# Query latents and attention's output gates with both input parts as one moving operand, and a convolution gate and its values in one weight group

## The chip, the cores and the metric

The kernel runs on one core of one Trainium2 chip. Its time is the device time of one execution in microseconds (us); several executions are run and their median is given. Five engines with queues of their own work side by side: TensorE (PE in the rows; PEld is its weight loads), VectorE (DVE), ScalarE (ACT), GpSimd (POOL, unused here) and SyncE (SP), which only issues DMAs.

## What is computed

Two blocks on 256 tokens of 2048 channels, all in float32. The first (attention with a recurrence, then an MLP) is not touched. The second has two layers, and each does this:

```python
z = h @ w_in[l]
q_lat, kv_lat, k_rope, mla_gate, conv_in, conv_gate = jnp.split(z, splits, axis=-1)
q = (rms_norm(q_lat, q_lat_g[l]) @ w_q_up[l]).reshape(b, s, N_HEADS, QK_DIM)
kv = (rms_norm(kv_lat, kv_lat_g[l]) @ w_kv_up[l]).reshape(b, s, N_HEADS, NOPE_DIM + V_DIM)
...
attn = causal_block_attention(q, k, v).reshape(b, s, D_MLA)
mla_out = attn * jax.nn.silu(mla_gate)
u_val, u_gate = jnp.split(conv_in + glu_b[l], 2, axis=-1)
u = u_val * jax.nn.sigmoid(u_gate)
u = causal_depthwise_conv(u, dw_w[l], dw_b[l])
u = jax.nn.silu(layer_norm(u, conv_ln_g[l], conv_ln_b[l]))
u = u @ w_pw[l] + b_pw[l]
conv_out = u * jax.nn.silu(conv_gate)
y = jnp.concatenate([mla_out, conv_out], axis=-1) @ w_out[l]
x = x + gate * y
```

q_lat has 512 channels (4 tiles of 128), mla_gate 1024 (8 tiles), u_gate and u_val 1024 each, conv_gate 1024; the convolution has 31 taps.

## The kernel before

Every float32 product is made of three: a number is split into a high part that TensorE takes exactly and the rest, and `high*high + high*low + low*high` is summed in PSUM. The input's parts are `HT[:, kt, 0]` and `HT[:, kt, 1]` (`HTh`, `HTl`); a weight's parts are `WH` and `WL`.

**Halves.** Weights arrive in chunks of up to 1 MB. Each chunk is worked on in halves of up to 128x1024 numbers, and the half is the unit of the whole kernel. ScalarE makes `WH` (line 1922), VectorE makes `WL = RAW - WH` (line 1084, called the split of that half here), TensorE multiplies. There are four buffers for each part, so the high part of half n+4 can begin when TensorE has finished half n. There are 636 halves in all and 130 in each layer of the second block; halves are numbered 0 to 129 within a layer here, also for the changed kernel.

**Two ways of multiplying.** `products` with `cols=4` (lines 578 to 580) has a half of 2 input tiles x 4 output tiles and issues three matmuls of 256 columns for each of these 8 pairs. `joint_products` (lines 630, 632) has 4 input tiles x 2 output tiles, and issues one matmul of 512 columns (both input parts against `WH`) and one of 256 (`HTh` against `WL`) for each pair. The two input parts then lie in two stretches of a bank, and have to be added: ScalarE copies one to SBUF (`second_part`, line 2570), and VectorE adds the other (`summed`, line 1080), 2 operations of 256 columns for each group of 2 tiles.

**The order of a layer** (`weight_course`): group of convolution gates 0 to 3 (halves 0 to 7), values 0 to 3 joint (8 to 15), key and value latents (16 to 23), query latents (24 to 31), `w_kv_up` (32 to 35), convolution gates 4 to 7 (36 to 43), their values (44 to 51), `w_q_up` (52 to 57, three groups of two halves), attention's output gates (58 to 73), the convolution's output gates joint (74 to 89), half of `w_out2` (90 to 97), `w_pw`, the rest of `w_out2`. Groups take two pairs of PSUM banks in turn, so a group's first matmul waits for whoever reads the group two before it.

**Side work** is cut into steps, the strands. `Course.beat` runs one step of every strand behind each half, on each engine by the same count: TensorE's step stands behind its half n, while VectorE's and ScalarE's step n stands ahead of their work for half n+4. So VectorE does step n between its splits of halves n+3 and n+4. The strands: `convolution` (VectorE's taps, line 1443, 3 or 4 to a step by `tap_steps`, and one start per tile by ScalarE, line 2142), `key_latents`, `query_latents`, `heads` (norms and rotation of keys and queries), `attend` (26 steps) and `channel_norm` (15 steps, starts when both convolution strands have ended). TensorE's small products of the strands take four further banks in turn (`small_bank`), and each waits until the reader of the bank's last content is done.

`glued` (line 1820) is VectorE's gated values: it reads a group of values in PSUM, adds the bias and multiplies by the gate. It releases the banks (`taken`).

## Time and profile before

| | |
|---|---|
| median of 3 executions | 1962.79 us (1962.68 to 1963.76) |
| the profiled execution | 1963.59 us, its span 1961.8 us |
| TensorE busy | 1939.5 us, 99% of the span |
| VectorE busy | 1525.5 us, 78% |
| ScalarE busy | 1069.1 us, 54% |
| granted TensorE clock | 1.0 throughout (2.4 GHz) |
| chain that ended last | 96% TensorE |

The profiler's span leaves out 1.8 us around the work. Shares are means over stages that differ: a layer of the second block takes about 409 us, the first from 1139 us and the second from 1548 us, and in some of its stretches VectorE is as busy as TensorE. The start of a ScalarE row on line 1922 that ended a wait for PE tells when TensorE finished the half four before it.

### The profile page before, as it was taken

To read this page: it belongs to the slowest core of one execution; us is meant where nothing else is said; L and a number is where in the kernel's file an instruction comes from. 1 tells how busy PE (TensorE), PEld (TensorE's weight loads), DVE (VectorE), ACT (ScalarE), POOL (GpSimd) and SP (SyncE) were. 2 spreads that over 40 slices of the span, in tenths; PEclk is the share of its full clock that TensorE was granted. 3 is DMA by queue.
4 is the path that set the end of the run, shared out by engine and by line. 5 is a ranking of instruction groups with operands and counts; after the bars stand their busy time and mean duration, and the time that the engine had idled before them with its cause. 6 is when DMAs were issued, how large, how long until landed. Compare 5 with 4: busy or idle time off the path is not lost.

```text
span 1961.8 us, 27925 instructions
## 1 busy us (share of the span) xinstructions
PE 1939.5 (99%) x11546; PEld 1683.0 (86%) x11546; DVE 1525.5 (78%) x2092; ACT 1069.1 (54%) x1545; POOL 0.2 (0%) x4
## 2 busy tenths in 40 slices
PE   7999999999999999999999999999999999999999
PEld 6888888888888888888888889999888899998887
DVE  6587776868887777888877567999966669999764
ACT  5474766465664433555543475554764566456742
POOL 0000000000000000000000000000000000000000
PEclk9999999999999999999999999999999999999999
DMA  7443445938889888989898734544455455454453
GB/s 283 153 164 124 139 151 200 358 134 296 332 337 335 331 332 331 340 321 338 330 334 331 254 125 165 187 168 139 163 188 181 147 193 173 151 172 135 172 194 123
DMA packets 63982, 442.59 MB, mean 226 GB/s; under 512 B 7248, under 2 KB 7536, under 8 KB 12400
## 3 DMA queue, kind: packets, MB, share of 16 engines
q1 hardware_dynamic: 61920, 434.30, 61.9%
q10 hardware_dynamic: 1936, 6.51, 1.0%
q8 instruction: 91, 1.49, 0.3%
q14 instruction: 35, 0.29, 0.0%
HBM read 438.67 MB, written 2.11 MB: 225 GB/s over the span
## 4 chain that ended last, share of the span: by engine, by line
PE 96%; DVE 2%; ACT 1%; DMA 0%; issue 0%; ACTq 0%; DVEq 0%
PE PS L630 22%; PE PS L632 11%; PE PS L509 11%; PE PS L511 11%; PE PS L510 11%; PE PS L578 7%; PE PS L579 7%; PE PS L580 7%; PE PS L501 6%; PE PS L657 1%; DMA X<-in_x 0%; DVE WL L1084 0%; DVE Y L1126 0%; ACT S L1985 0%; ACT WH L1922 0%
## 5 line engine op out<-in xcount | busy, mean ns | idle before, releaser
L1922 ACT ACTIVATE WH<-RAW 128x1024 fp32r<-128x1024 f32 (+1 forms) x636 | 663.6, 1049 | 752.3 <-PE PS L511 282.5
L1084 DVE TENSOR_TENSOR WL<-RAW,WH 128x1024 fp32r<-128x1024 f32 (+1 forms) x636 | 766.4, 1209 | 374.7 <-ACT WH L1922 373.4
L630 PE MATMUL PS<-HT,WH 128*128 128x512 f32 x1912 | 678.5, 398 | 0.0
L632 PE MATMUL PS<-HT,WL 128*128 128x256 f32 x1912 | 535.8, 280 | 0.0
L630 PEld LDWEIGHTS PS<-HT,WH 128*128 128x128 f32 x1912 | 358.6, 188 | 88.8 <-issue 7.2
L632 PEld LDWEIGHTS PS<-HT,WL 128*128 128x128 f32 x1912 | 361.3, 189 | 0.1
L578 PE MATMUL PS<-HT,WH 128*128 128x256 f32 x1008 | 291.2, 289 | 0.7 <-DVE HT L1135 0.4
L580 PE MATMUL PS<-HT,WL 128*128 128x256 f32 x1008 | 285.5, 283 | 0.0
L579 PE MATMUL PS<-HT,WH 128*128 128x256 f32 x1008 | 285.5, 283 | 0.0
L1093 DVE SCALAR_TENSOR_TENSOR RAW<-RAW,CB 128x2048 f32<-128x2048 f32 x96 | 219.3, 2284 | 0.0
L511 PE MATMUL PS<-WH,Ul 128*128 128x512 f32 x512 | 203.0, 396 | 0.0
L509 PE MATMUL PS<-WH,Uh 128*128 128x512 f32 x512 | 202.5, 396 | 0.0
L578 PEld LDWEIGHTS PS<-HT,WH 128*128 128x128 f32 x1008 | 193.4, 192 | 10.6 <-issue 7.8
L510 PE MATMUL PS<-WL,Uh 128*128 128x512 f32 x512 | 201.2, 393 | 0.0
L1443 DVE SCALAR_TENSOR_TENSOR UG<-UV,PK,UG 128x256 f32<-128x256 f32 x480 | 200.4, 478 | 0.2
L579 PEld LDWEIGHTS PS<-HT,WH 128*128 128x128 f32 x1008 | 193.6, 192 | 0.4
L580 PEld LDWEIGHTS PS<-HT,WL 128*128 128x128 f32 x1008 | 193.5, 192 | 0.0
L510 PEld LDWEIGHTS PS<-WL,Uh 128*128 128x128 f32 x512 | 96.1, 188 | 23.8
L511 PEld LDWEIGHTS PS<-WH,Ul 128*128 128x128 f32 x512 | 96.1, 188 | 23.7
L509 PEld LDWEIGHTS PS<-WH,Uh 128*128 128x128 f32 x512 | 96.1, 188 | 22.5
L509 PE MATMUL PS<-WH,HT 128*128 128x512 f32 x256 | 100.8, 394 | 0.0
L511 PE MATMUL PS<-WH,HT 128*128 128x512 f32 x256 | 99.8, 390 | 0.0
(317 smaller groups left out, 2026.7 us busy)
## 6 DMA issues: line engine op xcount, KB each, us to landing
RAW<-in_w_in SPq DMA_DIRECT2D x112, 1024.0 KB, 4.8
RAW<-in_ada_w SPq DMA_DIRECT2D x96, 1024.0 KB, 6.3
RAW<-in_w_up SPq DMA_DIRECT2D x64, 1024.0 KB, 5.8
RAW<-in_w_down SPq DMA_DIRECT2D x64, 1024.0 KB, 5.7
RAW<-in_w_out SPq DMA_DIRECT2D x48, 1024.0 KB, 4.8
RAW<-in_w_pw SPq DMA_DIRECT2D x8, 1024.0 KB, 4.8
RAW<-in_w_in SPq DMA_DIRECT2D x8, 768.0 KB, 4.2
RAW<-in_w_q_up SPq DMA_DIRECT2D x6, 1024.0 KB, 4.8
```

What stands on the lines that cost most here:

```text
L509: e.matmul(out, sh, mh, start=st, stop=False, skip_group_check=True)
L510: e.matmul(out, sh, ml, start=False, stop=False, skip_group_check=True)
L511: return e.matmul(out, sl, mh, start=False, stop=final, skip_group_check=True)
L578: e.matmul(out, sh, ah, start=first and i % 2 == 0, stop=False, skip_group_check=True)
L579: e.matmul(out, sh, al, start=False, stop=False, skip_group_check=True)
L580: op = e.matmul(out, sl, ah, start=False, stop=final, skip_group_check=True)
L630: e.matmul(bk[i][:, 0:512], wh[:, at], m["HT"][:, kt, :, :].rearrange("p a t -> p (a t)"), start=kt == 0, stop=False, skip_group_check=True)
L632: op = e.matmul(bk[i][:, 0:256], wl[:, at], HTh[:, kt, :], start=False, stop=kt == n.kts - 1, skip_group_check=True)
L1084: e.tensor_tensor(m[f"WL{j % NHL}"][:, 0:nk * w], m[f"RAW{i % NRAW}"][:, k0 * w:(k0 + nk) * w], m[f"WH{j % NHL}"][:, 0:nk * w].bitcast(F32 ...
L1093: e.scalar_tensor_tensor(raw[:, :], raw[:, :], 1.0, m["CB"][:, :], ALU.mult, ALU.mult, accum_out=mod[:, k:k + 1]).then_inc(signals["ada"], 1)
L1443: e.scalar_tensor_tensor(UG[:, c, :], UV[:, c, j:j + 256], dw[:, c, j:j + 1], UG[:, c, :], ALU.mult, ALU.add).then_inc(signals[name], 1)
L1922: e.activation(m[f"WH{j % NHL}"][:, 0:nk * w], m[f"RAW{i % NRAW}"][:, k0 * w:(k0 + nk) * w], ACT.Copy).then_inc(signals["high"], 1)
```

## The change

The input weights of a layer are grouped anew. A group of 512 columns now holds the gates of two channel tiles and the values of the same two (`GLU`, groups 0, 6 and 7); tiles 2 and 3 have two joint groups, gates and values (`GLU_JOINT`). The query latents are two joint groups in place of one plain group of four tiles, attention's output gates four joint groups in place of two plain ones. The number of halves stays, and so do their bytes. The parts of a joint group are added by `second_part` and `summed` as before. The convolution's first strand starts behind half 8 instead of behind half 16, with tiles 0 and 1, and takes up 2 and 3 from its turn 7; the second starts behind half 44 instead of 52, with tiles 4 and 5, and takes up 6 and 7 from its turn 10. The channel norm's step 10 waits until the last input product is through.

```diff
-GLU_VALUES, GLU_GATES, Q_LATENT, KV_LATENT, MLA_GATES, CONV_GATES = ((0, 1), 5), (2, 6), 3, 4, (7, 8), (9, 10, 11, 12)
-LAYER_JOINT = GLU_VALUES[0] + CONV_GATES
+GLU, GLU_JOINT, Q_LATENT, KV_LATENT, OUT_GATES = (0, 6, 7), (1, 2), (3, 4), 5, tuple(range(8, 16))
+LAYER_JOINT = GLU_JOINT + Q_LATENT + OUT_GATES
...
     def tap_steps(self, L, c0):
-        yield range(4)
-        n, turn = 4, 0
-        while n < 124:
-            k = min(3 if c0 == 0 and turn < SLOW_TURNS else 4, 124 - n)
-            yield range(n, n + k)
-            n, turn = n + k, turn + 1
+        later = 7 if c0 == 0 else 10
+        done = [0] * 4
+        for turn in range(99):
+            taps = []
+            if turn in (1, later):
+                taps = [(0, c0 + c) for c in ((0, 1) if turn == 1 else (2, 3))]
+            for _ in range(3 if c0 == 0 and later < turn <= later + SLOW_TURNS else 4):
+                c = min(range(4 if turn > later else 2), key=lambda c: done[c])
+                if turn > 1 and done[c] < 30:
+                    done[c] += 1
+                    taps.append((done[c], c0 + c))
+            yield taps
+            if sum(done) == 120:
+                return
...
@@ tensor_program
-        for g in GLU_VALUES[0]:
+        taps = [course.start(convolution(L, 0))]
+        for g in GLU_JOINT:
             joint_products(group[f"w_in2_{L}", g], h)
-        taps = [course.start(convolution(L, 0))]
         products(group[f"w_in2_{L}", KV_LATENT], *hidden, h, cols=3)
         side_k = course.start(key_latents(L))
-        products(group[f"w_in2_{L}", Q_LATENT], *hidden, h, cols=4)
+        for g in Q_LATENT:
+            joint_products(group[f"w_in2_{L}", g], h)
...
-        for g in (GLU_GATES[1], GLU_VALUES[1]):
-            products(group[f"w_in2_{L}", g], *hidden, h, cols=4)
+        products(group[f"w_in2_{L}", GLU[1]], *hidden, h, cols=4)
         taps.append(course.start(convolution(L, 4)))
+        products(group[f"w_in2_{L}", GLU[2]], *hidden, h, cols=4)
...
-        for g in MLA_GATES:
-            products(group[f"w_in2_{L}", g], *hidden, h, cols=4)
-        for g in CONV_GATES:
+        for g in OUT_GATES:
             joint_products(group[f"w_in2_{L}", g], h)
+        flags.add(("inputs", L))
...
@@ vector_program
+        def glued(g, c0, gates):
             n = group[f"w_in2_{L}", g]
+            dve.wait_ge("half_done", n.done)
+            dve.wait_ge("uz", L + 1)
+            dve.wait_ge("u_sig", 4 * L + gates)
+            for c in range(c0, c0 + 2):
+                op = e.scalar_tensor_tensor(UV[:, c, 30:286], bank[2 * n.pair + 1][:, 256 * (c - c0):256 * (c - c0) + 256],
+                                            pk(f"glu_b{L}")[:, c:c + 1], UG[:, c, :], ALU.add, ALU.mult)
+            op.then_inc(signals["taken"], 1)
...
+        n = group[f"w_in2_{L}", GLU[2]]
+        for j, _ in course.begin(n):
+            if j == n.first + 1:
+                glued(GLU[1], 4, 3)
         norm = course.start(channel_norm(L, taps))
         course.drain(side_q)
         for g in range(3):
-            course.group(group[f"w_q_up_{L}", g])
+            n = group[f"w_q_up_{L}", g]
+            for j, _ in course.begin(n):
+                if g == 0 and j == n.first + 1:
+                    glued(GLU[2], 6, 4)
...
@@ scalar_program
-        for k, g in enumerate(CONV_GATES):
+        for k, g in enumerate(OUT_GATES):
             n = group[f"w_in2_{L}", g]
             for j, _ in course.begin(n):
-                if k == 2 and j == n.first + 2:
-                    gates_done(0)
-            second_part(n, CG[:, 2 * k:2 * k + 2, :])
+                if k and k % 2 == 0 and j == n.first + 2:
+                    gates_done(k // 2 - 1)
+            second_part(n, (MG, CG)[k // 4][:, 2 * (k % 4):2 * (k % 4) + 2, :])
```

**First place: VectorE around the start of `w_q_up`.** `UV<-PS,PK,UG` is `glued`, `UG<-UV,PK,UG` the taps, `WL<-RAW,WH` the splits. Before, the first row is the split of half 54:

```order
L1084 TENSOR_TENSOR WL<-RAW,WH 128x1024 [waits high]
L1820 SCALAR_TENSOR_TENSOR UV<-PS,PK,UG 128x256 [waits stored,uz,half_done]
L1820 SCALAR_TENSOR_TENSOR UV<-PS,PK,UG 128x256 x3
L1443 SCALAR_TENSOR_TENSOR UG<-UV,PK,UG 128x256 [waits taps0] x4
L1084 TENSOR_TENSOR WL<-RAW,WH 128x1024 [waits high] x2
```

In the changed kernel, the second split here is that of half 56 and the last that of half 57:

```order
L1095 TENSOR_TENSOR WL<-RAW,WH 128x1024 [waits high]
L1460 SCALAR_TENSOR_TENSOR UG<-UV,PK,UG 128x256 [waits taps1] x4
L1095 TENSOR_TENSOR WL<-RAW,WH 128x1024 [waits high]
L1837 SCALAR_TENSOR_TENSOR UV<-PS,PK,UG 128x256 [waits u_sig,half_done]
L1837 SCALAR_TENSOR_TENSOR UV<-PS,PK,UG 128x256
L1460 SCALAR_TENSOR_TENSOR UG<-UV,PK,UG 128x256 [waits taps1] x4
L1095 TENSOR_TENSOR WL<-RAW,WH 128x1024 [waits high]
```

The gated values that free a pair of banks for the second group of `w_q_up` stood behind the split of half 54 and now stand behind that of half 56; on TensorE the group that waits for them begins with half 54 in both.

**Second place: VectorE where the queries' heads end and attention begins.** `QN<-QN,PK,PS` and `QP<-QP,PS` are the last two steps of `heads`, `S<-PS,CN` and `MX<-S` attention's scores. Before (the second split is that of half 71, the last that of 72):

```order
L1525 SCALAR_TENSOR_TENSOR QN<-QN,PK,PS 128x512 [waits h_wide]
L1528 TENSOR_TENSOR QP<-QP,PS 64x256 x2
L1443 SCALAR_TENSOR_TENSOR UG<-UV,PK,UG 128x256 [waits taps1] x4
L1084 TENSOR_TENSOR WL<-RAW,WH 128x1024 [waits high]
L1525 SCALAR_TENSOR_TENSOR QN<-QN,PK,PS 128x512 [waits h_wide]
L1528 TENSOR_TENSOR QP<-QP,PS 64x256 x2
L1548 SCALAR_TENSOR_TENSOR S<-PS,CN 128x384 [waits a_score] x2
L1554 TENSOR_REDUCE MX<-S 128x1 [waits a_in]
L1554 TENSOR_REDUCE MX<-S 128x1
L1443 SCALAR_TENSOR_TENSOR UG<-UV,PK,UG 128x256 [waits taps1] x4
L1084 TENSOR_TENSOR WL<-RAW,WH 128x1024 [waits high]
```

and in the changed kernel:

```order
L1091 TENSOR_TENSOR Y<-PS,Y 128x256 [waits joint_low] x2
L1542 SCALAR_TENSOR_TENSOR QN<-QN,PK,PS 128x512 [waits h_wide]
L1545 TENSOR_TENSOR QP<-QP,PS 64x256 x2
L1460 SCALAR_TENSOR_TENSOR UG<-UV,PK,UG 128x256 [waits taps1] x4
L1095 TENSOR_TENSOR WL<-RAW,WH 128x1024 [waits high]
L1542 SCALAR_TENSOR_TENSOR QN<-QN,PK,PS 128x512 [waits h_wide]
L1545 TENSOR_TENSOR QP<-QP,PS 64x256 x2
L1565 SCALAR_TENSOR_TENSOR S<-PS,CN 128x384 [waits a_score] x2
L1571 TENSOR_REDUCE MX<-S 128x1 [waits a_in]
L1571 TENSOR_REDUCE MX<-S 128x1
L1460 SCALAR_TENSOR_TENSOR UG<-UV,PK,UG 128x256 [waits taps1] x4
L1095 TENSOR_TENSOR WL<-RAW,WH 128x1024 [waits high]
```

Two sums of a joint group (`Y<-PS,Y`) stand there besides all that stood there before; the same pair comes in ahead of the splits of halves 67, 71, 75 and 79.

**Third place: TensorE where the channel norm begins.** `PS<-UG,CN` is its first sum, `PS<-CN,S` and `PS<-VT,V` are a step of attention. Before, behind half 83:

```order
L632 MATMUL PS<-HT,WL 128x256
L501 MATMUL PS<-UG,CN 32x256 [waits taps1,taps0]
L501 MATMUL PS<-UG,CN 32x256 x7
L630 MATMUL PS<-HT,WH 128x512 [waits split]
```

and in the changed kernel, behind half 76:

```order
L641 MATMUL PS<-HT,WL 128x256
L925 MATMUL PS<-CN,S 128x128 [waits a_probs,a_pt]
L925 MATMUL PS<-CN,S 128x128 x2
L510 MATMUL PS<-VT,V 128x256 [waits a_out]
L510 MATMUL PS<-VT,V 128x128
L510 MATMUL PS<-UG,CN 32x256 [waits taps1,taps0,a_in]
L510 MATMUL PS<-UG,CN 32x256 x7
L639 MATMUL PS<-HT,WH 128x512 [waits split]
```

The norm's sum moved ahead by seven halves, into the middle of attention's steps, and it now takes the bank of a pair of scores: it waits for `a_in`, VectorE's reading of the fifth head's scores (`S<-PS,CN`), which stands behind the split of half 79.

## Rows read from the trace of the kernel before

**Rows 1.** The page's first part: busy time, share of the span and instructions.

```profile
PE 1939.5 (99%) x11546; PEld 1683.0 (86%) x11546; DVE 1525.5 (78%) x2092; ACT 1069.1 (54%) x1545; POOL 0.2 (0%) x4
```

**Rows 2.** The page's fourth part: the chain that ended last, by engine.

```profile
PE 96%; DVE 2%; ACT 1%; DMA 0%; issue 0%; ACTq 0%; DVEq 0%
```

**Rows 3.** Windows of the first layer; PE, PEld, DVE, ACT, POOL busy, clock, DMA.

```profile
1229.00:1268.00 39.00, 39.00 (x293) 35.29 (x292) 35.84 (x63) 22.66 (x31) 0.00 (x0) 1.00 0.61 212
1268.00:1308.00 40.00, 40.00 (x330) 38.97 (x330) 39.69 (x74) 16.66 (x21) 0.00 (x0) 1.00 0.41 142
1309.00:1413.00 104.00, 104.00 (x762) 93.84 (x761) 103.72 (x207) 61.00 (x104) 0.00 (x0) 1.00 0.45 154
```

**Rows 4.** Timeline of PE, query latents as plain products: start, us, operation.

```profile
1223.70 0.28 PE L578 MATMUL PS<-HT,WH 128*128 128x256 f32 x1
1223.82 0.28 PE L579 MATMUL PS<-HT,WH 128*128 128x256 f32 x1
1223.94 0.28 PE L580 MATMUL PS<-HT,WL 128*128 128x256 f32 x1
1224.06 0.28 PE L578 MATMUL PS<-HT,WH 128*128 128x256 f32 x1
```

**Rows 5.** Timeline of PE in a joint group (values 2 and 3).

```profile
1189.55 0.39 PE L630 MATMUL PS<-HT,WH 128*128 128x512 f32 x1
1189.78 0.28 PE L632 MATMUL PS<-HT,WL 128*128 128x256 f32 x1
1189.90 0.39 PE L630 MATMUL PS<-HT,WH 128*128 128x512 f32 x1
```

**Rows 6.** Timeline of DVE behind half 15: two sums, and the split of 19.

```profile
1194.77 0.79 DVE L1080 TENSOR_TENSOR UV<-PS,UV 128x256 f32<-128x256 f32 x2 [1.39 <-ACT UV L2570]
...
1196.20 0.95 DVE L1084 TENSOR_TENSOR WL<-RAW,WH 128x768 fp32r<-128x768 f32 x1
```

**Rows 7.** Timeline of DVE ahead of half 41's split: split of 40, then keys' rotation.

```profile
1253.77 1.23 DVE L1084 TENSOR_TENSOR WL<-RAW,WH 128x1024 fp32r<-128x1024 f32 x1 [0.58 <-ACT WH L1922]
...
1257.63 0.34 DVE L1499 TENSOR_SCALAR KV<-KV,PK 128x256 f32<-128x256 f32 x1
```

**Rows 8.** Timeline of ACT there: TensorE has finished halves 38 and 39.

```profile
1258.37 1.06 ACT L1922 ACTIVATE WH<-RAW 128x1024 fp32r<-128x1024 f32 x1 [2.48 <-PE PS L580]
...
1262.36 1.06 ACT L1922 ACTIVATE WH<-RAW 128x1024 fp32r<-128x1024 f32 x1 [2.41 <-PE PS L580]
```

**Rows 9.** Timeline of DVE around `w_q_up`'s start: gated values, splits of 55, 56.

```profile
1302.80 1.22 DVE L1084 TENSOR_TENSOR WL<-RAW,WH 128x1024 fp32r<-128x1024 f32 x1
1304.05 1.66 DVE L1820 SCALAR_TENSOR_TENSOR UV<-PS,PK,UG 128x256 f32<-128x256 f32 x4
1305.62 1.67 DVE L1443 SCALAR_TENSOR_TENSOR UG<-UV,PK,UG 128x256 f32<-128x256 f32 x4
1307.20 1.22 DVE L1084 TENSOR_TENSOR WL<-RAW,WH 128x1024 fp32r<-128x1024 f32 x1
1308.81 1.23 DVE L1084 TENSOR_TENSOR WL<-RAW,WH 128x1024 fp32r<-128x1024 f32 x1 [0.38 <-ACT WH L1922]
```

**Rows 10.** Timeline of ACT there: TensorE has finished halves 51 and 55.

```profile
1300.89 1.06 ACT L1922 ACTIVATE WH<-RAW 128x1024 fp32r<-128x1024 f32 x1 [1.76 <-PE PS L580]
...
1312.41 1.06 ACT L1922 ACTIVATE WH<-RAW 128x1024 fp32r<-128x1024 f32 x1 [0.78 <-PE PS L580]
```

**Rows 11.** Timeline of DVE: split of half 72, split of 79 and the scores behind it.

```profile
1366.15 1.22 DVE L1084 TENSOR_TENSOR WL<-RAW,WH 128x1024 fp32r<-128x1024 f32 x1
...
1388.19 1.22 DVE L1084 TENSOR_TENSOR WL<-RAW,WH 128x1024 fp32r<-128x1024 f32 x1
1389.33 1.01 DVE L1548 SCALAR_TENSOR_TENSOR S<-PS,CN 128x384 f32<-128x384 f32 x2
```

**Rows 12.** Timeline of ACT: TensorE has finished halves 68, 76 and 78.

```profile
1360.02 1.06 ACT L1922 ACTIVATE WH<-RAW 128x1024 fp32r<-128x1024 f32 x1 [4.38 <-PE PS L580]
...
1388.93 1.06 ACT L1922 ACTIVATE WH<-RAW 128x1024 fp32r<-128x1024 f32 x1 [0.97 <-PE PS L632]
...
1395.46 1.06 ACT L1922 ACTIVATE WH<-RAW 128x1024 fp32r<-128x1024 f32 x1 [1.23 <-PE PS L632]
```

**Rows 13.** Timeline of PE: attention's step behind half 76, then half 77 begins.

```profile
1388.67 0.49 PE L916 MATMUL PS<-CN,S 128*128 128x128 f32 x3
1388.99 0.82 PE L501 MATMUL PS<-VT,V 128*128 128x256 f32 x4
1389.57 0.48 PE L630 MATMUL PS<-HT,WH 128*128 128x512 f32 x1
```

More of the change, by code:

```diff
@@ L933, in channel_norm @@
         for n in range(15):
+            while n == 10 and ("inputs", L) not in flags:
+                yield
             if n == 0:
                 b = small()
-                pe.wait_ge("taps0", 124 * L + 124)
-                pe.wait_ge("taps1", 124 * L + 124)
+                pe.wait_ge("taps0", 120 * L + 120)
+                pe.wait_ge("taps1", 120 * L + 120)
                 spread_sum(b, lambda i: UG[:, i, :]).then_inc(signals["n_sum"], 1)
@@ L1582, in channel_norm @@
         for n in range(15):
+            while n == 10 and ("inputs", L) not in flags:
+                yield
             if n in (0, 2, 6, 8):
@@ L1795, in vector_program @@
         UV, UG = m["UV"], m["UG"]
-        CG = Y[:, 1, :].rearrange("p (h t) -> p h t", h=8)
+        MG, CG = (Y[:, i, :].rearrange("p (h t) -> p h t", h=8) for i in range(2))
         def summed(g, part):
@@ L1826, in vector_program @@
         course.pace = 1
-        course.group(group[f"w_in2_{L}", GLU_GATES[0]])
+        course.group(group[f"w_in2_{L}", GLU[0]])
         course.pace = 99
-        a, b = GLU_VALUES[0]
+        taps = [course.start(convolution(L, 0))]
+        a, b = GLU_JOINT
+        n = group[f"w_in2_{L}", a]
+        for j, _ in course.begin(n):
+            if j == n.first + 1:
+                glued(GLU[0], 0, 1)
+        n = group[f"w_in2_{L}", b]
+        for j, _ in course.begin(n):
+            if j == n.first + 1:
+                summed(a, UG[:, 2:4, :])
+            if j == n.done - 1:
+                summed(b, UV[:, 2:4, 30:286])
+                gated()
@@ L1830, in vector_program @@
+        course.group(group[f"w_in2_{L}", KV_LATENT])
+        side_k = course.start(key_latents(L))
+        a, b = Q_LATENT
         course.group(group[f"w_in2_{L}", a])
@@ L1833, in vector_program @@
             if j == n.first + 1:
-                summed(a, UV[:, 0:2, 30:286])
-                gated(0)
+                summed(a, m["QN"][:, 0:2, :])
             if j == n.done - 1:
-                summed(b, UV[:, 2:4, 30:286])
-                gated(2)
-        taps = [course.start(convolution(L, 0))]
-        course.group(group[f"w_in2_{L}", KV_LATENT])
-        side_k = course.start(key_latents(L))
-        course.group(group[f"w_in2_{L}", Q_LATENT])
+                summed(b, m["QN"][:, 2:4, :])
         side_q = course.start(query_latents(L))
@@ L1848, in vector_program @@
         side = course.start(attend(L))
-        course.group(group[f"w_in2_{L}", GLU_GATES[1]])
-        glued(GLU_VALUES[1], 4)
+        course.group(group[f"w_in2_{L}", GLU[1]])
         taps.append(course.start(convolution(L, 4)))
+        n = group[f"w_in2_{L}", GLU[2]]
+        for j, _ in course.begin(n):
+            if j == n.first + 1:
+                glued(GLU[1], 4, 3)
         norm = course.start(channel_norm(L, taps))
@@ L1861, in vector_program @@
                 if before is not None and j == n.first + 1:
-                    at = 2 * CONV_GATES.index(before)
-                    summed(before, CG[:, at:at + 2, :])
-            before = next((g for g in CONV_GATES if group[f"w_in2_{L}", g] is n), None)
+                    k = OUT_GATES.index(before)
+                    at = 2 * (k % 4)
+                    summed(before, (CG if k >= 4 else MG)[:, at:at + 2, :])
+            before = next((g for g in OUT_GATES if group[f"w_in2_{L}", g] is n), None)
+            if before == OUT_GATES[-1]:
+                flags.add(("inputs", L))
         course.drain(side, norm)
@@ L2267, in channel_norm @@
         for n in range(15):
+            while n == 10 and ("inputs", L) not in flags:
+                yield
             if n == 1:
@@ L2318, in store_R @@
             op = e.activation(dst(i), bank[2 * n.pair + i][:, :], ACT.Copy)
-        op.then_inc(signals["stored"], 1)
-    def store_biased(n, dst, func, bias):
-        act.wait_ge("half_done", n.done)
-        for f in range(4):
-            op = e.activation(dst(f), bank[2 * n.pair + f // 2][:, 256 * (f % 2):256 * (f % 2) + 256], func,
-                              bias=bias[:, f:f + 1])
         op.then_inc(signals["stored"], 1)
@@ L2558, in scalar_program, with gate_pair @@
         glu = pk(f"glu_b{L}")
-        def conv_gate(g, f0):
+        def gate_pair(g, c0):
             n = group[f"w_in2_{L}", g]
-            course.group(n)
-            store_biased(n, lambda f: UG[:, f0 + f, :], ACT.Sigmoid, glu[:, 8 + f0:12 + f0])
+            act.wait_ge("half_done", n.done)
+            for c in range(c0, c0 + 2):
+                op = e.activation(UG[:, c, :], bank[2 * n.pair][:, 256 * (c - c0):256 * (c - c0) + 256], ACT.Sigmoid,
+                                  bias=glu[:, 8 + c:9 + c])
+            op.then_inc(signals["u_sig"], 1)
         def second_part(n, part, func=ACT.Copy, bias=None):
@@ L2587, in scalar_program @@
         side_k = course.start(key_latents(L))
-        n = group[f"w_in2_{L}", Q_LATENT]
-        course.group(n)
-        store_T(n, QN[:, 0:4, :])
+        for k, g in enumerate(Q_LATENT):
+            n = group[f"w_in2_{L}", g]
+            for j, _ in course.begin(n):
+                if j == n.done - 1:
+                    second_part(n, QN[:, 2 * k:2 * k + 2, :])
         side_q = course.start(query_latents(L))
```

124 lines of the change are left out of this document (64 added, 60 removed).

## Prediction

> **What bounds the kernel now.** The shares of busy time come first [rows 1]: TensorE is busy for 99% of the span. The chain that ended last [rows 2] says the same of the order of events: 96% of it is TensorE. So a saving on TensorE counts in full, as long as nobody else becomes late. Whether somebody does is read from the windows [rows 3]: in the stretch from 1309 to 1413 us VectorE is busy for 103.72 of 104 us, from 1268 to 1308 us for 39.69 of 40. TensorE doesn't wait there, since VectorE works ahead: it has made the low part of a half some time before TensorE starts on it. I call this time the lead. It is the quantity of this case, and it is read from two timelines: the end of VectorE's split, and ScalarE's rows, which tell when TensorE finished a half. For half 56 the split ends at 1308.81 + 1.23 = 1310.04 [rows 9], and half 55 is done at 1312.4 [rows 10]: a lead of 2.4 us. For half 79 it is 1395.46 - (1388.19 + 1.22) = 6.0 us [rows 11, 12]. For half 72: half 68 is done at 1360.0 [rows 12], halves 69 to 71 are plain (2.88 us each, below), so half 72 starts at 1368.6, and its split ends at 1367.4 [rows 11]: a lead of only 1.2 us. A lead falls by VectorE's new work and by TensorE's saved time alike.
>
> **What TensorE saves.** A plain pair of tiles takes three matmuls that start 0.12 us apart, 0.36 us [rows 4]. A joint one takes 1189.90 - 1189.55 = 0.35 us, more exactly 0.346 (1.04 us for three in that timeline) [rows 5]. A half has 8 pairs: 2.88 us against 2.77, so 0.11 us. The change turns 24 halves of a layer from plain to joint (8 of the query latents, 16 of attention's gates); the gates and values of the convolution keep their count of both kinds. Saved: 24 x 0.11 = 2.7 us a layer, 5.4 us in all.
>
> The Trainium skill (TensorE: Matmul & The Clock Gate, section Back-to-back issue gap) gives an isolated gap of N/2.4 + 2.5 ns. By that the three matmuls cost 327.5 ns and the two 325 ns, so an estimate from the page is a saving of 2.5 ns for each of 384 pairs, 1.0 us in place of 5.4. The rows show 14 ns a pair, and the sum goes by them.
>
> **What it adds elsewhere.** Weight bytes and DMAs stay. ScalarE copies the second parts; it is busy for 61.00 of 104 us in the tightest stretch [rows 3], which hides them. VectorE adds the parts: 12 more tiles a layer. Two sums take 0.79 us from start to end [rows 6], 0.7 us up to the next start. Gating takes 6 reads of PSUM and one product in place of 4 and two, which is even. The taps keep their 120 and move: four of them (4 x 0.4 = 1.6 us, from 1.67 us for four [rows 9]) now stand between the sums behind half 15 and the split of half 19. At that point VectorE waits for the sums' operand anyway [rows 6], so this comes off its lead directly.
>
> **First new wait, the keys' rotation behind half 38.** TensorE's rotation needs VectorE's gain, which ends at 1257.97 [rows 7]; TensorE is there at 1258.3 [rows 8]. The margin is 0.3 us at a lead for half 40 of 1262.3 - 1255.0 = 7.3 us. The new lead: 7.3, plus the 2.9 us that VectorE idles up to there out of the 3.2 us of its first window [rows 3], less 1.6 for taps, 0.9 for eight joint halves, 1.4 for two pairs of sums: 6.3 us. With the banks of the latents' sum, which `w_kv_up`'s second group waits for behind the split of half 34, I take 0.6 us a layer (0 to 1.2).
>
> **Second, and the largest: the second group of `w_q_up`.** Its first half is 54, and it uses the banks that the gated values release (first place in the order). Before, these stood behind the split of half 54 and ended at 1304.05 + 1.66 = 1305.7 [rows 9], 0.9 us before TensorE came at 1300.9 + 2 x 2.88 = 1306.6 [rows 10]. Now they stand behind the split of half 56. Its lead is 2.4 us, plus 0.8 us as only two of the four gated tiles stand ahead of it since the strand began, plus up to 0.4 us for the idle time that ScalarE's late start caused [rows 9], less 0.2 from upstream: 3.3 us. So that split ends 3.3 us before half 56 starts, which is 5.76 - 3.3 = 2.5 us after TensorE is ready for half 54. Two gated tiles of 0.4 us each and the signal follow: TensorE waits 3.4 us. Bounds: with the longest lead that four buffers allow (the high part of half 56 can only begin when half 52 is done, and 1.06 + 1.23 us of ScalarE and VectorE follow [rows 9, 10]) the wait is 0.5 us; with a lead of 2.4 it is 4.3.
>
> **Third, attention's stretch.** The second wait gives VectorE its lead back, so behind it I count 0.5 us more than before at half 66. From there to the split of half 79 VectorE never idles [rows 3], and has four more pairs of sums (2.7 us), while TensorE's ten joint halves take 1.1 us less. The lead at half 79 becomes 6.0 + 0.5 - 2.7 - 1.1 = 2.7 us if nobody waits. TensorE must wait, though: the norm's first sum now stands behind half 76 and takes a bank whose scores VectorE reads behind the split of half 79 (third place). In the trace TensorE would be there at 1389.57 [rows 13], and the first scores are read at 1389.33 + 0.5 = 1389.9 [rows 11], so even with a lead of 6.0 it would wait 0.3 us; with 2.7 it waits 3.6. Part of this comes earlier, at half 72, whose lead of 1.2 doesn't cover two pairs of sums and the joint halves (1.4 + 1.4 us, less the 0.5 and 0.8 of regained lead), and behind half 74, where the softmax's result is late; what is waited there is not waited again. So 3.6 us for the stretch, between 0.4 (the lead as before) and 4.8 (nothing regained).
>
> **The sum.** A layer: -2.7 + 0.6 + 3.4 + 3.6 = +4.9 us. Two layers, whose order is the same: +9.8. The profiled execution took 1963.6 us, so 1973.4; it lies 0.8 us over the median, so the median becomes 1972.6 us. The ends: 1963.6 - 5.4 + 2 x (0 + 0.5 + 0.4) = 1960.0 and 1963.6 - 5.4 + 2 x (1.2 + 4.3 + 4.8) = 1978.8, before the 0.8 us.
>
> **The rivals.**
> - *Faster: VectorE keeps its lead.* If its lead at halves 56 and 79 is near what the buffers allow, the waits are the lower ends, 0.9 us a layer, and the saving stands: 1959.2 us. For it: the taps start eight halves earlier, when VectorE idles between splits (1.39 us ahead of the sums [rows 6]). Against it: both convolution strands still run without a gap, and from 1268 us on VectorE is full. It decides at a lead of 5.4 us for half 56. Chance 0.11.
> - *No difference: the waits cost about what the matmuls save*, say 1.7 us behind the gated values and 1.0 in attention's stretch: 2 x (2.7 - 2.7) = 0, 1962.8 us. It needs half of my lead arithmetic to be wrong in one direction. Chance 0.13.
> - *Slower still: ScalarE is drawn in.* The changed kernel makes SiLU of attention's gates between exponentials, behind a wait for VectorE's sums, and a wait of ScalarE delays the high parts behind it, these the splits. With 4 us a layer on top it is 1981 us. Against it: ScalarE is busy for under 60% there [rows 3]. Chance 0.12.
> - *TensorE saves only 1.0 us.* In the trace's terms it is joint pairs that start 0.357 us apart in place of 0.346. With the same waits that is 1972.6 + 4.4 = 1977 us. Against it stand the rows themselves [rows 5]. Chance 0.02. The Trainium skill's page named above is where this would come from.
>
> **How the numbers follow.** The sum is the likeliest case, 0.62, and gives the time, 1972.6 us. The range of 1961 to 1982 us takes in its bounds, the case of no difference and the nearer part of the slower one; the faster case and what lies beyond 1982 are left out, somewhat under 0.2 together. A measurement of this kernel can tell about 0.2% (3.9 us) from no change. Slower by more: 0.62 + 0.12 + 0.02 = 0.76; the same: 0.13; faster: 0.11.
>
> **What would show it.** In the profile after: joint matmuls pairwise 0.346 us apart in latents and gates; a gap on TensorE of some 3.4 us at the first matmul of `w_q_up`'s second group, ended by VectorE's gated values; a second gap, of 1 to 3.6 us, at the norm's first sum, ended by the scores' reading, with smaller ones at half 72 and behind half 74; the first window of a layer without idle time on VectorE. TensorE's busy share falls. I am wrong if the gap at `w_q_up` is under 1 us, which would say that VectorE's lead was longer than I worked out, or if the gaps are there and the total is lower, which would say that a plain half costs more than 2.88 us somewhere that I haven't looked.

## The result, and the profile after

The changed kernel takes 1978.99 us (median of 4 runs, 1978.07 to 1979.31), the kernel before beside it 1962.85 us: a ratio of 1.0079, 95% interval 1.0067 to 1.0092. It is slower by 16.1 us, where 9.8 were forecast; the time of 1972.6 us was 6.4 us too low and the range of 1961 to 1982 holds the result. The profiled execution has a span of 1977.5 us, 15.7 us longer than before.

The page's first part, then the shares of the chain that ended last, answer to [rows 1, 2]:

```profile
PE 1943.0 (98%) x11162; PEld 1667.1 (84%) x11162; DVE 1533.8 (78%) x2118; ACT 1072.6 (54%) x1561; POOL 0.2 (0%) x4
```

```profile
PE 78%; DVE 18%; ACT 2%; issue 1%; DMA 0%; ACTq 0%; DVEq 0%
```

TensorE has 384 matmuls fewer and is busy for longer than before. VectorE's part of the chain has grown from 2% to 18%. Where TensorE waited, in the first layer (who waited for whom: us in total, times, longest), after the change:

```profile
PE PS L587 <- DVE UV L1837: 3.8, 1, 3.8
PE PS L510 <- DVE S L1565: 1.8, 1, 1.8
PE PS L510 <- DVE Y L1091: 1.6, 1, 1.6
PE PS L573 <- ACT VT L1998: 0.9, 1, 0.9
PE PS L925 <- ACT S L2274: 0.4, 1, 0.4
```

The same view and stretch of the kernel before:

```profile
PE PS L501 <- DVE Y L1080: 1.6, 1, 1.6
PE PS L564 <- ACT VT L1965: 0.9, 1, 0.9
```

Lines 1091 and 573 of after are lines 1080 and 564 of before, so three waits are new. The largest is at the second group of `w_q_up` (half 54), for the gated values of line 1837. Around it, VectorE's timeline (start, us, operation), then TensorE's:

```profile
1305.17 1.22 DVE L1095 TENSOR_TENSOR WL<-RAW,WH 128x1024 fp32r<-128x1024 f32 x1
1306.31 1.67 DVE L1460 SCALAR_TENSOR_TENSOR UG<-UV,PK,UG 128x256 f32<-128x256 f32 x4
1307.89 1.22 DVE L1095 TENSOR_TENSOR WL<-RAW,WH 128x1024 fp32r<-128x1024 f32 x1
1309.14 0.88 DVE L1837 SCALAR_TENSOR_TENSOR UV<-PS,PK,UG 128x256 f32<-128x256 f32 x2
```

```profile
1310.08 0.58 PE L587 MATMUL PS<-QLh,WH 128*128 128x256 f32 x1 [3.80 <-DVE UV L1837]
...
1310.88 0.41 PE L587 MATMUL PS<-QLh,WH 128*128 128x256 f32 x1
1311.10 0.41 PE L588 MATMUL PS<-QLl,WH 128*128 128x256 f32 x1
...
1315.72 0.28 PE L589 MATMUL PS<-QLh,WL 128*128 128x256 f32 x1
1315.83 0.28 PE L587 MATMUL PS<-QLh,WH 128*128 128x256 f32 x1
```

TensorE is ready at 1310.08 - 3.80 = 1306.28, the split of half 56 ends at 1309.11, the two gated values at 1310.02. That is the wait that was forecast. What follows was not: the matmuls then start 0.213 us apart on average (the pair shown, 1310.88 to 1311.10, a little more) and only from 1315.7 on 0.12 us apart as in [rows 4]. The 26 that start between 1310.08 and 1315.72 take 5.64 us, where 26 x 0.12 = 3.1 would do. Windows of that stretch (busy us of PE, PEld, DVE, ACT, POOL, then the granted clock, the DMA engines' share, GB/s):

```profile
1303.00:1306.20 3.20, 3.20 (x28) 3.07 (x26) 3.20 (x6) 1.06 (x1) 0.00 (x0) 1.00 0.66 276
1306.20:1308.80 2.60, 0.08 (x1) 0.00 (x0) 2.60 (x6) 2.03 (x3) 0.00 (x0) 1.00 0.54 129
1308.80:1310.00 1.20, 0.00 (x0) 0.00 (x0) 1.17 (x4) 0.00 (x0) 0.00 (x0) 0.50 1.02 430
1310.00:1315.60 5.60, 5.53 (x26) 5.53 (x27) 4.32 (x10) 1.09 (x2) 0.00 (x0) 0.50 0.43 139
1315.60:1318.00 2.40, 2.40 (x22) 2.40 (x22) 1.25 (x2) 1.06 (x1) 0.00 (x0) 1.00 0.47 198
```

TensorE was busy throughout, then idle; 2.5 us into the idle time the granted clock fell to 0.5, its level of 1.2 GHz, and stayed there for 6.8 us, of which 5.5 are work. [Rows 3] have 1.00 everywhere, since before the change TensorE never stood still there. In the second layer the wait is 3.8 us too, and the clock falls 2.4 us into it, again for 6.8 us. So the place costs 3.8 + 2.6 = 6.4 us a layer. The Trainium skill (TensorE: Matmul & The Clock Gate, section Back-to-back issue gap) gives an isolated gap of N/1.2 ns at the lower clock, by which an estimate for 256 columns is 213 ns; the 0.213 us of the trace agrees.

The second and third new waits are in attention's stretch. At the norm's first sum behind half 76, first TensorE's row, then VectorE's:

```profile
1397.45 1.07 PE L510 MATMUL PS<-UG,CN 128*32 128x256 f32 x16 [1.82 <-DVE S L1565]
```

```profile
1396.84 1.02 DVE L1565 SCALAR_TENSOR_TENSOR S<-PS,CN 128x384 f32<-128x384 f32 x2
```

The bank's scores are read from 1396.84 on, behind the split of half 79, and TensorE is there 1.8 us ahead of the first one's end. It is the wait that was worked out from [rows 11, 13], shorter than the 3.6 us counted there. Behind half 74 it waits for the softmax's result, 0.43 us of the 0.6 us that half 75 loses:

```profile
1385.47 0.52 PE L925 MATMUL PS<-CN,S 128*128 128x128 f32 x3 [0.43 <-ACT S L2274]
```

The ends of the halves in both traces, subtracted, give the whole account. For the first layer, in us (the second differs by at most 0.1 in any line):

| halves | after less before | what it is |
|---|---|---|
| 0 to 53 | -0.4 | eight joint halves |
| 54, 55 | +6.5 | wait 3.8, slow clock 2.6 |
| 56 to 74 | -0.9 | sixteen joint halves |
| 75 | +0.6 | softmax's result late |
| 76 to 92 | +2.1 | wait 1.8 at the norm's sum |
| sum | +7.8 | two layers: 15.5 of 15.7 |

### The profile page after: what moved, and what is told of

It is laid out like the page before. It is cut to its first block, busy times and chain, and to the rows that moved or that the text cites. A ratio compares the mean times of both kernels' runs of the same rounds, so it can differ in the third digit from the quotient of the medians.

```text
span 1977.5 us, 27203 instructions
## 1 busy us (share of the span) xinstructions
PE 1943.0 (98%) x11162; PEld 1667.1 (84%) x11162; DVE 1533.8 (78%) x2118; ACT 1072.6 (54%) x1561; POOL 0.2 (0%) x4
## 4 chain that ended last, share of the span: by engine, by line
PE 78%; DVE 18%; ACT 2%; issue 1%; DMA 0%; ACTq 0%; DVEq 0%
PE PS L639 22%; PE PS L641 11%; PE PS L520 11%; PE PS L518 11%; PE PS L519 11%; DVE UG L1460 7%; DVE WL L1095 6%; PE PS L510 4%; PE PS L587 2%; PE PS L588 2%; PE PS L589 2%; ACT WH L1955 1%; PE PS L666 1%; DVE Y L1091 0%; DMA X<-in_x 0%
## 5 line engine op out<-in xcount | busy, mean ns | idle before, releaser
L639 PE MATMUL PS<-HT,WH 128*128 128x512 f32 x2296 | 817.5, 399 | 0.0
L639 PEld LDWEIGHTS PS<-HT,WH 128*128 128x128 f32 x2296 | 430.8, 188 | 111.2 <-issue 12.3
L587 PE MATMUL PS<-HT,WH 128*128 128x256 f32 x624 | 180.1, 289 | 0.7 <-DVE HT L1146 0.4
L588 PE MATMUL PS<-HT,WH 128*128 128x256 f32 x624 | 176.9, 283 | 0.0
L587 PEld LDWEIGHTS PS<-HT,WH 128*128 128x128 f32 x624 | 119.9, 192 | 6.1 <-DVE WL L1095 2.9
L588 PEld LDWEIGHTS PS<-HT,WH 128*128 128x128 f32 x624 | 120.1, 192 | 0.2
```

Of the source, the lines that this page charges most:

```text
L587: e.matmul(out, sh, ah, start=first and i % 2 == 0, stop=False, skip_group_check=True)
L588: e.matmul(out, sh, al, start=False, stop=False, skip_group_check=True)
L639: e.matmul(bk[i][:, 0:512], wh[:, at], m["HT"][:, kt, :, :].rearrange("p a t -> p (a t)"), start=kt == 0, stop=False, skip_group_check=True)
```

## The experiments

All times are medians, with the ratio to the kernel before and its 95% interval. The kernel before stands at 1962.8 to 1963.7 us beside them, the changed kernel at 1979.0 us beside a before of 1962.85; a difference from the changed kernel is therefore good to about 1 us. Cuts in the code are marked with `...`; of an edit in several programs the tensor program's lines are shown.

**The wait and the clock at half 54.** First the gated values two splits earlier, where they stood before:

```diff
         n = group[f"w_in2_{L}", GLU[2]]
         for j, _ in course.begin(n):
             if j == n.first + 1:
                 glued(GLU[1], 4, 3)
+            if j == n.done - 1:
+                glued(GLU[2], 6, 4)
...
         for g in range(3):
-            n = group[f"w_q_up_{L}", g]
-            for j, _ in course.begin(n):
-                if g == 0 and j == n.first + 1:
-                    glued(GLU[2], 6, 4)
+            course.group(group[f"w_q_up_{L}", g])
```

> The changed kernel, but the gated values of tiles 6 and 7 stand behind VectorE's split of half 54, as before the change, and not behind that of half 56. My theory: in the changed kernel TensorE loses 6.4 us a layer at half 54, 3.8 as a wait for these values and 2.6 because it then runs at a granted clock of 0.5 for 6.8 us. Both go. Not all comes back: in the changed kernel VectorE idles 4.1 us a layer behind half 57, being as far ahead as the four buffers allow, and its lead at half 72 is 0.3 us; with 6.4 us less for TensorE the lead is 2 us short at half 72, and TensorE waits there. Net 4.4 us a layer: 1979.0 - 8.8 = 1970.2 us. Rival, the lead has room: the full 12.8 come back, 1966.2 us. Rival, only the wait of 3.4 us that I forecast matters and VectorE sets the pace throughout: all is taken again in attention's stretch, 1979 us.

Measured: 1968.68 us (ratio to before 1.0034, 1.0022 to 1.0047), 10.3 us less than the changed kernel. Its waits in the first layer (the stretch listed begins just behind the 1.6 us wait of both kernels, which is still there):

```profile
PE PS L510 <- DVE S L1565: 1.8, 1, 1.8
PE PS L510 <- DVE HS L1534: 1.2, 1, 1.2
PE PS L573 <- ACT VT L1997: 0.9, 1, 0.9
PE PS L925 <- ACT S L2273: 0.4, 1, 0.4
```

The wait and the slow clock are gone, 6.4 us a layer, and 1.5 us come back, at half 65 (queries' rotation, the second row) and half 68. I had put 2 us at half 72: right in kind, wrong in place. One of the five executions took 1973.55 us at a mean granted clock of 0.998, where the profiled one had 1.00 throughout; only one execution of a kernel is profiled, so where its lower clock lay isn't known.

One split earlier instead of two (`j == n.first` in place of `j == n.first + 1`):

> The changed kernel, but the gated values of tiles 6 and 7 stand one split earlier, behind that of half 55. In the trace of the changed kernel that split ends at 1306.39 and TensorE is ready at 1306.28, so with 0.88 us for the two gated values and 0.1 for the signal TensorE waits 1.1 us. My theory: a wait of that length leaves the clock at 1.0 (so did the wait of 1.8 us in attention's stretch), so 3.8 - 1.1 + 2.6 = 5.3 us a layer go at this place, of which 0.9 come back at half 72: 1979.0 - 8.8 = 1970.2 us, the same as with no wait at all. Rival, each wait at this place lowers the clock: 2.7 us a layer, 1973.6 us.

Measured: 1968.78 us (1.0032, 1.002 to 1.0043), like the run before and 1.4 under the forecast. The wait is there, the clock is 1.00 behind it, and the matmuls go on at 0.12 us. TensorE's row, and the window that in the changed kernel had 0.50:

```profile
1306.49 0.38 PE L587 MATMUL PS<-QLh,WH 128*128 128x256 f32 x1 [1.10 <-DVE UV L1837]
```

```profile
1308.80:1315.60 6.80, 6.80 (x59) 6.80 (x59) 6.80 (x14) 3.22 (x5) 0.00 (x0) 1.00 0.52 186
```

So a wait of 1.1 us here costs nothing in the end: VectorE gets the time, and the 1.5 us at halves 65 and 68 shrink by about as much. To take the clock apart from the wait, TensorE was kept busy while it waited, with `keep_warm`, small products of constants that both kernels already have at other places:

```diff
         for g in range(3):
+            if g == 1:
+                keep_warm(28)
             products(group[f"w_q_up_{L}", g], tile_of("QLh"), tile_of("QLl"), lambda kt: ("l_l", 2 * L + 2), cols=4)
```

> The changed kernel with 28 more small matmuls on TensorE (128x128 constants into a free bank, nobody reads them) ahead of the second group of w_q_up in each layer. They take 28 x 0.12 = 3.4 us of the 3.8 us that TensorE waits there. My theory: the granted clock falls because TensorE stood idle. Then half 54 still waits to the same moment, but the clock stays at 1.0: 2.6 us a layer come back, which VectorE's 4.1 us of idle time behind half 57 cover: 1979.0 - 5.2 = 1973.8 us, with no stretch at 0.5 in the records. Rival, the clock falls for another reason (the work around it, the moment in the layer): it still falls, and the time is 1979 us or, with the small matmuls behind their operand, somewhat more.

Measured: 1978.61 us (1.0081, 1.0068 to 1.0093), no gain, yet not by the rival's reason. TensorE's rows:

```profile
1305.29 6.41 PE L510 MATMUL PS<-CN 128*128 128x128 f32 x56
1311.46 0.36 PE L587 MATMUL PS<-QLh,WH 128*128 128x256 f32 x1
```

Each small product is two matmuls, so the filling took 6.2 us and outlasted the wait by 2.4, about what the clock gave back (2.6): from 1311.66 on the matmuls run at 0.12 us. The filling was too long by a factor of two. With `keep_warm(15)`:

> The changed kernel with 15 small matmuls of constants on TensorE ahead of the second group of w_q_up. In the run with 28 the rows showed two matmuls for each (float32 operands) at 0.11 us, 6.2 us in all, so it filled more than the wait of 3.8 us; the clock stayed at 1.0 and what it gave went into the longer filling. With 15 it is 30 matmuls, 3.3 us. My theory, that the clock falls because TensorE stands idle for that long: the place costs 3.8 us a layer in place of 6.4, the clock stays at 1.0, and VectorE's idle time behind half 57 covers the difference: 1979.0 - 5.2 = 1973.8 us. Rival, TensorE's pause of 0.5 us behind the small matmuls or their kind of work is enough for the slow clock: 1979 us.

Measured: 1974.38 us (1.0057, 1.0045 to 1.007), 4.6 less than the changed kernel, 5.2 forecast. TensorE's rows and the window:

```profile
1305.18 3.51 PE L510 MATMUL PS<-CN 128*128 128x128 f32 x30
1309.12 0.39 PE L587 MATMUL PS<-QLh,WH 128*128 128x256 f32 x1 [0.43 <-DVE UV L1839]
```

```profile
1308.80:1315.60 6.80, 6.48 (x54) 6.48 (x55) 6.71 (x14) 2.57 (x4) 0.00 (x0) 1.00 0.53 183
```

The operand comes as late as ever (3.9 us after the last product ahead of it); only most of TensorE's idleness is gone, and with it the slow clock. That shows the cause. In between, with `keep_warm(4)`:

> The changed kernel with 4 small products of constants (8 matmuls of 0.11 us, 0.9 us) ahead of the second group of w_q_up, so that TensorE stands idle for 2.9 us there in place of 3.8. So far waits of 3.8 us were followed by 3.4 or 6.8 us at a granted clock of 0.5, and waits of 1.9 us and less by none. The case between them decides what a wait costs: if the clock stays at 1.0, the place costs 3.8 us in place of 6.4, as with 15 products: 1974.4 us. If it falls behind 2.9 us as well, nothing changes or a little (3.4 us at 0.5 in place of 6.8): 1977.5 to 1979 us. I expect the latter, with 0.6 against 0.4.

Measured: 1976.58 us (1.0065, 1.0051 to 1.0079).

```profile
1309.27 0.39 PE L587 MATMUL PS<-QLh,WH 128*128 128x256 f32 x1 [2.92 <-DVE UV L1839]
```

```profile
1308.80:1315.60 6.80, 6.33 (x40) 6.34 (x41) 5.22 (x12) 2.15 (x3) 0.00 (x0) 0.75 0.55 188
```

After 2.9 us idle the clock falls too, for 3.4 us in both layers (mean 0.75 over the window). Somewhat less was lost than I gave. Here the clock falls only once TensorE is at work again, in the first layer 0.4 us behind the end of the wait:

```profile
1309.30:1309.60 0.30, 0.30 (x2) 0.30 (x3) 0.30 (x2) 0.30 (x1) 0.00 (x0) 1.00 1.03 437
1309.70:1313.00 3.30, 3.30 (x18) 3.30 (x17) 3.30 (x7) 0.64 (x2) 0.00 (x0) 0.50 0.12 30
```

**Which part of the change costs what.** Attention's gates as plain groups again (two groups with `products`, stored by ScalarE with SiLU, no `summed`):

```diff
+        for g in MLA_GATES:
+            products(group[f"w_in2_{L}", g], *hidden, h, cols=4)
         for g in OUT_GATES:
             joint_products(group[f"w_in2_{L}", g], h)
```

> The changed kernel with one part undone: attention's output gates are two plain groups again (ScalarE stores them, VectorE sums nothing for them). TensorE loses 16 x 0.055 = 0.9 us a layer by it, VectorE gets 4 pairs of sums back, 2.8 us. My theory: the wait and the slow clock at half 54 stay (6.4 us a layer, nothing ahead of it changes), and in attention's stretch the waits of 1.8 us at half 77 and 0.6 at half 75 go: 1979.0 - 2 x (2.4 - 0.9) = 1976.0 us. Rival, these waits come from the norm's place and its bank alone and not from the sums: 1979.0 + 1.8 = 1980.8 us.

Measured: 1974.81 us (1.006, 1.0047 to 1.0073), below the forecast. Both waits of attention's stretch are gone (-0.6 at half 75, -1.9 at half 77 in each layer); the rest is the slow clock, which lasted 3.4 us in one layer of the profiled run. So the sums of these gates are needed for those waits, and the joint form of the gates loses more than it saves: 2.5 us against 0.9 a layer. The wait at half 77 needs the norm's place as well; it also goes when that alone is moved (below).

The query latents as a plain group again:

```diff
-        for g in Q_LATENT:
-            joint_products(group[f"w_in2_{L}", g], h)
+        products(group[f"w_in2_{L}", Q_LATENT], *hidden, h, cols=4)
```

> The changed kernel with another part undone: the query latents are one plain group again. TensorE loses 8 x 0.055 = 0.4 us a layer, VectorE gets two pairs of sums back, 1.4 us, ahead of w_q_up. My theory: VectorE's lead at half 56 grows by both, 1.8 us, so TensorE waits 2.0 us at half 54 in place of 3.8. Whether the clock falls behind a wait of 2.0 us is open: if it does (6.8 us at 0.5, 2.6 us lost) the time is 1979.0 - 2 x 1.4 = 1976.3 us, if it doesn't, 1971.1 us. I expect the latter, as the wait of 1.9 us at half 77 left the clock at 1.0. Rival, VectorE's sums of the latents don't reach as far as half 56 (the lead at halves 42 to 45 is long enough to hide them): wait and clock stay, and the time is 1979.0 + 0.9 = 1979.9 us.

Measured: 1977.58 us (1.0075, 1.0062 to 1.0087). My theory fell and the rival held. The wait is 3.7 us, as long as ever; what was gained is a slow clock of 3.4 us instead of 6.8. VectorE's window around half 44, first in this run, then in the changed kernel:

```profile
1280.00:1292.00 12.00, 12.00 (x102) 12.00 (x102) 11.09 (x21) 4.52 (x7) 0.00 (x0) 1.00 0.51 171
```

```profile
1280.00:1292.00 12.00, 12.00 (x101) 11.90 (x100) 11.10 (x22) 4.50 (x7) 0.00 (x0) 1.00 0.46 157
```

VectorE idles there for 0.9 us in both. It has worked so far ahead that it must wait for a buffer, and whatever it lost or won before is forgotten at that point: with the latents plain, its lead is 1.1 us longer than in the changed kernel at half 34, 0.5 at half 40 and 0.1 at half 44, and the wait at half 54 is 0.1 us shorter.

Both parts plain, so that only the new grouping with its order is left:

> The changed kernel with latents and attention's gates both plain again: what is left of the change is the new grouping of the convolution's gates and values with their order, and nothing on TensorE is saved. My theory: the two undone parts act at different places, so the differences add: the run with plain gates gave -4.2 us, that with plain latents is forecast at -7.9 (clock kept) or -2.7 (clock lost), together 1966.9 or 1972.1 us. That is above the kernel before, as the wait at w_q_up's second group comes from where the gated values stand. Rival, the regrouping alone is free: 1962.8 us.

Measured: 1974.85 us (1.0058, 1.0045 to 1.0072), above both forecasts. So the two joint parts cost the changed kernel 4.1 us net, and the regrouping with its order alone costs 11.9 us over the kernel before, by the one wait and the slow clock that comes with it (6.8 us in the first layer, 3.4 in the second):

```profile
PE PS L587 <- DVE UV L1838: 7.3, 2, 3.7
```

**The norm's sum.** In the changed kernel, the norm three halves later, by three steps that do nothing at its start on each engine:

```diff
         while any(strand in course.strands for strand in taps):
             yield
+        for _ in range(3):
+            yield
```

> The changed kernel, but the channel norm starts three halves later, so that its first sum stands behind half 79 and takes a bank that nobody holds, in place of a bank with scores that VectorE reads behind the split of half 79. My theory: the wait of 1.8 us behind half 76 goes (its small matmuls stay, 1.07 us), and VectorE's lead of 7 to 8 us behind it covers that: 1979.0 - 3.6 = 1975.4 us. Rival, VectorE sets the pace there and another wait takes its place: 1979 us.

Measured: 1973.02 us (1.0051, 1.0037 to 1.0065). The wait is gone and none took its place: -2.1 us in the first layer. The rest of the 6.0 us less than the changed kernel is partly a slow clock of 3.4 us in place of 6.8 in the second layer of the profiled run. Together with the gated values at their old place:

> Gated values of tiles 6 and 7 behind the split of half 54, and the channel norm three halves later. Each alone gave 1968.7 and 1973.0 us. My theory: at half 77 the two work apart, since VectorE's lead there came out the same with and without the wait at w_q_up (4.2 us in both traces): 1968.7 less 2 x 2.1 (what a layer lost in the first layer's rows of the run with the later norm) = 1964.5 us. Rival, VectorE has no time to give and another wait takes the place of the norm's: 1968.7 us.

Measured: 1965.31 us (1.001, 1.0001 to 1.0018), 0.8 us above the forecast. What is left in its first layer, beside the 1.6 us wait of both kernels:

```profile
PE PS L510 <- DVE HS L1536: 1.3, 1, 1.3
PE PS L573 <- ACT VT L2001: 0.9, 1, 0.9
PE PS L925 <- ACT S L2277: 0.6, 1, 0.6
```

**VectorE's taps at other places.** With the gated values at their old place, the second strand's taps slower early on:

```diff
-            for _ in range(3 if c0 == 0 and later < turn <= later + SLOW_TURNS else 4):
+            for _ in range(3 if c0 == 0 and later < turn <= later + SLOW_TURNS or c0 and 2 <= turn < 18 else 4):
```

> Gated values of tiles 6 and 7 behind the split of half 54, and the second strand of the convolution with 3 taps in each of its turns 2 to 17 and 4 behind them, in place of 4 throughout: it ends 4 halves later, where VectorE idles, and the channel norm with it. The taps, the sums and the bytes are the same in number. My theory is that all that is left of the loss is VectorE's lead in halves 54 to 76: the 15 taps of 0.4 us that go behind half 76 give it 6 us. Then the waits of 1.2 us at half 65, 0.3 at 68, 0.6 at 75 and 1.8 at 77 all go: 1968.7 - 2 x 3.9 - what is left of norm's bank, about 0.3 a layer = 1960.3 us, under the kernel before by what TensorE saves (1.2 us a layer in the rows). Rival, the lead can't be carried over since four buffers cap it near 8 to 10 us at half 64 (the lead at half 72 then stays short): only the waits at 65 and 77 go, 1962.6 us.

Measured: 1963.75 us (1.0001, 0.9992 to 1.001). The wait at half 65 is gone, those at halves 75 and 81 stay. VectorE's windows of this run, halves 54 to 64 and then 64 to 75:

```profile
1305.00:1340.00 35.00, 35.00 (x237) 30.01 (x236) 31.50 (x55) 20.10 (x28) 0.00 (x0) 1.00 0.54 181
1340.00:1380.00 40.00, 39.38 (x234) 32.55 (x233) 39.72 (x80) 19.77 (x35) 0.00 (x0) 1.00 0.37 127
```

Ahead of half 64 it idles for 3.5 us, behind it for 0.3: the taps were taken from the wrong stretch. So, the gated values still at their old place, the slow turns were moved to where it never idles:

```diff
-            for _ in range(3 if c0 == 0 and later < turn <= later + SLOW_TURNS else 4):
+            for _ in range(3 if c0 == 0 and later < turn <= later + SLOW_TURNS or c0 and turn in (8, 9, 10, 11, 18, 19, 20, 21, 22, 23, 24, 25) else 4):
```

> Gated values of tiles 6 and 7 behind the split of half 54, and 3 taps in place of 4 in turns 8 to 11 and 18 to 25 of the second strand, which are those behind the splits of halves 55 to 58 and 65 to 72; the strand ends 3 halves later than in the changed kernel and the norm's first sum stands behind half 79. In the run with the slower taps in turns 2 to 17 the lead reached 10 us at half 64 and was 0.1 us at half 72 all the same: what VectorE saves ahead of half 64 is lost at the cap that four buffers set, and 0.8 us at half 75 and 0.5 at half 81 stayed. My theory: taps left out behind half 65 count in full at half 72 to 76 (8 x 0.4 = 3.2 us), four ahead of it are enough for half 65 (short by 1.3 us there), and no wait is left: 1963.75 - 2 x 1.3 = 1961.1 us, perhaps 1960.3. Rival, the wait at half 75 is ScalarE's own (its exponentials between high parts) and not VectorE's lead: 1962.7 us.

Measured: 1959.92 us, median of 11, ratio 0.9986, 95% interval 0.9977 to 0.9995: faster than both kernels. Its first part of the page, and what is left of TensorE's waits in its first layer:

```profile
PE 1934.6 (99%) x11162; PEld 1660.8 (85%) x11162; DVE 1532.0 (78%) x2118; ACT 1072.4 (55%) x1561; POOL 0.2 (0%) x4
```

```profile
PE PS L510 <- DVE Y L1091: 1.6, 1, 1.6
PE PS L573 <- ACT VT L1997: 0.9, 1, 0.9
```

These two stand in the kernel before as well. None of the three new waits is there. By the ends of the halves a layer is 1.5 us shorter than before the change. That is what the change brings when nobody is late, about the 1.4 us that the joint halves save in the changed kernel's rows; the rival, that the wait at half 75 is ScalarE's own, fell.

## Why the prediction came out as it did

- **What bounds the kernel, and the lead as the quantity to watch:** right. All three new waits are for VectorE's work, the one behind half 74 by way of ScalarE's softmax, and each goes when VectorE's work is placed or sized otherwise. Of the signs named, the two gaps, the smaller one behind half 74, VectorE's full first window and TensorE's lower share (98%) came; a gap at half 72 and the spacing of 0.346 us throughout did not.
- **What TensorE saves, 2.7 us a layer:** about 1.4 (1.35 and 1.43). The step took 0.346 us a pair from one group [rows 5] for all of them. The changed halves run at another spacing, in a group of the query latents:

```profile
1224.64 0.40 PE L639 MATMUL PS<-HT,WH 128*128 128x512 f32 x1
1224.88 0.28 PE L641 MATMUL PS<-HT,WL 128*128 128x256 f32 x1
1224.99 0.40 PE L639 MATMUL PS<-HT,WH 128*128 128x512 f32 x1
1225.24 0.28 PE L641 MATMUL PS<-HT,WL 128*128 128x256 f32 x1
1225.36 0.40 PE L639 MATMUL PS<-HT,WH 128*128 128x512 f32 x1
1225.59 0.28 PE L641 MATMUL PS<-HT,WL 128*128 128x256 f32 x1
1225.70 0.40 PE L639 MATMUL PS<-HT,WH 128*128 128x512 f32 x1
```

  Three pairs take 1225.70 - 1224.64 = 1.06 us, 0.353 each, and a half 2.83 us in place of 2.77. The trace of before already had both: of its 239 joint halves 175 run without other work or a wait between their pairs, 89 at 0.346 to 0.347 us and 86 at 0.353 to 0.354. Both layers together save 2.8 us, between the sum's 5.4 and the 1.0 of the rival (pairs at 0.357), nearer to the rival, which got 0.02. Its source, the isolated gap in the Trainium skill (TensorE: Matmul & The Clock Gate, section Back-to-back issue gap), fits neither spacing: both lie above the 325 ns that N/2.4 + 2.5 ns gives for the two matmuls.
- **The keys' rotation, 0.6 us:** no wait. The lead at half 40 came out at 6.8 us, not 6.3, and the margin held. The term should have been nothing.
- **`w_q_up`'s second group, 3.4 us:** the wait is 3.8, for the reason given. The lead of half 56 is 2.9 us, not 3.3. What VectorE did ahead of half 44 doesn't count, since its lead is cut there (the run with plain latents shows it); the 0.2 us for it should have been nothing, and the 1.2 us counted as regained were 0.5. What was missing altogether is the slow clock, 2.6 us: the sum had no term for what TensorE does after a wait. This is the failed step, and most of the 6.4 us by which the time was too low: 2 x 2.6 = 5.2.
- **Attention's stretch, 3.6 us:** 2.7 measured (0.6 and 2.1). Place and bank were right. VectorE regained more than the 0.5 us counted, since half 54 took TensorE 6.4 us more: its lead at half 64 is 10.0 us, against 8.1 before. With that loss taken away, 1.5 us appeared at halves 65 and 68, together 4.2 us: the forecast's size, with its parts elsewhere. The step at half 72 was wrong in place; the lead there did fall to 0.3 us and was not overdrawn. It also counted ten joint halves behind half 66 where there are eight, 0.2 us.
- **The sum:** -1.3 + 0 + 6.4 + 2.7 = 7.8 in the first layer against 4.9. The saving was 1.4 too large and the clock's 2.6 was missing; the keys (0.6 too much), the wait (0.4 too little) and attention's stretch (0.9 too much) take 1.1 off that, so two of the wrong terms hid a part of the loss by luck. It is luck as well that the range holds the result: 1979.0 lies 1 us above the sum's own upper end (1978.8 - 0.8 = 1978.0), and the range reached further only for the rival "slower still". That had the right direction with the wrong mechanism: ScalarE wasn't drawn in beyond the 0.6 us at half 75.

What stays open: what sets which of the two spacings a joint half gets. It is the same in both layers for most halves, but halves 58 and 59 of the changed kernel have the slower one in the first layer and the faster one in the second. No run was made for it.

## What to carry to other kernels

When a change puts an operand behind later work of a helper engine, price the wait, and then what the waiting engine does after it: here the wait of 1.8 us cost about its length, one of 2.9 or 3.8 cost 1.6 to 2.6 us more by TensorE's clock. VectorE's lead was capped by its buffers, so only its work since it last idled counted; time was to be taken from it in the stretch where it never idles, not earlier. A small saving on the bounding engine pays only when the helper's added work has a place: the same change lost 0.8% as it was and won 0.14% with the gated values where they had been and twelve taps moved.
